# One interleaved program for projection, attention and output of each mixer in the second block

## The reference, cut to what matters

```
proj = rms_norm(x, n1) @ w_in_l                     # 1024 -> 2560
qa, ka, va, qd, kd, vd, qc, kc, vc = split(proj)    # 256x3, 384x3, 384, 128, 128
qa, ka, qd, kd, qc, kc: rms_norm per head of 64     # with gains
qd, kd: rotary on 16 of 64; qc, kc: axial rotary on all 64
out_a = softmax(qa ka^T + bias from rpb) va         # 4 heads, neighbourhood
out_d = softmax(qd kd^T + log of multiplicity) vd   # 6 heads, dilated windows
out_c = softmax(qc kc^T) vc                         # 6 heads over 2 key heads
mix = concat(rms_norm(out_a), rms_norm(out_d), rms_norm(out_c))
x = x + mix @ w_out_l                               # 1024 -> 1024
```

## Time and profile before

| | |
|---|---|
| median of 3 runs | 1798.05 us (1797.01 to 1801.28) |
| the profiled execution: its time | 1802.4 us |
| the profiled execution: its span | 1800.6 us |
| mean granted clock of TensorE in it | 0.971 of full |
| busy share: TensorE, VectorE, ScalarE, GpSimd | 93%, 57%, 47%, 8% |

### The profile page before, as it was taken

How to read it: one execution, slowest core, us unless ns; L and a number is a source line. 1 busy time by engine, 2 the same in 40 slices (tenths; PEclk the granted TensorE clock), 3 DMA queues, 4 the chain that set the end, 5 groups by cost and what they waited for, 6 DMA issues and landing times.

```text
span 1800.6 us, 28794 instructions
## 1 busy us (share of the span) xinstructions
PE 1683.3 (93%) x11689; PEld 1526.4 (85%) x11689; DVE 1024.3 (57%) x1303; ACT 844.1 (47%) x1185; POOL 152.2 (8%) x190
## 2 busy tenths in 40 slices
PE   7999997899999999998999998968999997899998
PEld 7999885799989999886689997946999987579997
DVE  6444555544455444668654445675655566666654
ACT  5344465444435443436544444564544454644443
POOL 0000011000000000230000002530000038000000
PEclk9999997999999999999999999989999998999999
DMA  7555441355545555432045555511545564025452
GB/s 267 187 186 187 162 153 61 133 194 186 186 164 188 185 181 181 154 118 71 25 176 187 183 179 139 201 48 47 187 166 197 182 180 163 1 100 190 177 188 92
DMA packets 40546, 276.85 MB, mean 154 GB/s; under 512 B 5505, under 2 KB 6290, under 8 KB 7570
## 3 DMA queue, kind: packets, MB, share of 16 engines
q1 hardware_dynamic: 39010, 271.00, 42.5%
q0 software_dynamic: 1456, 4.72, 1.7%
HBM read 274.65 MB, written 1.05 MB: 153 GB/s over the span
## 4 chain that ended last, share of the span: by engine, by line
PE 80%; DVE 9%; ACT 5%; POOL 3%; issue 2%; DMA 0%; SPq 0%; POOLq 0%; DVEq 0%; ACTq 0%
PE bank L661 19%; PE bank L642 14%; PE bank L644 14%; PE bank L643 14%; PE bank L622 5%; PE bank L573 3%; PE bank L574 3%; PE bank L575 3%; DVE w_lo L1356 2%; ACT prob L1178 1%; POOL proj L500 1%; ACT work L1064 1%; DVE prob L1536 1%; PE bank L718 1%; ACT w_hi L1054 1%
## 5 line engine op out<-in xcount | busy, mean ns | idle before, releaser
L1356 DVE TENSOR_TENSOR w_lo<-raw,w_hi 128x2048 fp32r<-128x2048 f32 x255 | 587.4, 2308 | 533.9 <-ACT w_hi L1054 533.2
L1054 ACT ACTIVATE w_hi<-raw 128x2048 fp32r<-128x2048 f32 x255 | 487.3, 1917 | 552.2 <-PE bank L644 404.0
L642 PE MATMUL bank<-xt_hi,w_hi 128*128 128x256 f32 x2112 | 599.8, 284 | 5.7 <-DVE xt_lo L1388 5.7
L644 PE MATMUL bank<-xt_hi,w_lo 128*128 128x256 f32 x2112 | 598.2, 283 | 0.0
L643 PE MATMUL bank<-xt_lo,w_hi 128*128 128x256 f32 x2112 | 598.1, 283 | 0.0
L642 PEld LDWEIGHTS bank<-xt_hi,w_hi 128*128 128x128 f32 x2112 | 405.6, 192 | 9.4 <-issue 5.0
L643 PEld LDWEIGHTS bank<-xt_lo,w_hi 128*128 128x128 f32 x2112 | 405.7, 192 | 2.5
L644 PEld LDWEIGHTS bank<-xt_hi,w_lo 128*128 128x128 f32 x2112 | 405.7, 192 | 0.0
L661 PE MATMUL bank<-w_hi,h_hi 128*128 128x512 f32 x528 | 208.3, 395 | 0.2
L661 PE MATMUL bank<-w_hi,h_lo 128*128 128x512 f32 x528 | 208.5, 395 | 0.0
L661 PE MATMUL bank<-w_lo,h_hi 128*128 128x512 f32 x528 | 208.2, 394 | 0.0
(11 more groups left out here) (301 smaller groups left out, 1635.2 us busy)
## 6 DMA issues: line engine op xcount, KB each, us to landing
raw<-in_stream SPq DMA_DIRECT2D x255, 1024.0 KB, 4.9
work<-in_rpb POOLq DMA_DIRECT2D x32, 64.0 KB, 3.7
X<-in_x SPq DMA_DIRECT2D x2, 512.0 KB, 4.0
prob<-in_cmp_w POOLq DMA_DIRECT2D x1, 1024.0 KB, 5.3
O<-in_cmp_w POOLq DMA_DIRECT2D x1, 1024.0 KB, 7.0
out<-X SPq DMA_DIRECT2D x1, 1024.0 KB, 4.0
cst<-in_consts SPq DMA_DIRECT2D x1, 776.0 KB, 5.9
O<-in_final_gain POOLq DMA_DIRECT2D x1, 512.0 KB, 4.2
```

What stands on the lines that cost most here:

```text
L642: pe.matmul(o, w_hi[:, sl, cols], xt_hi[:, k, :], start=(k == 0), stop=False)
L644: ins = pe.matmul(o, w_lo[:, sl, cols], xt_hi[:, k, :], start=False, stop=(k == KD - 1))
L1054: act.activation(w_hi[:, sl, :], raw[:, sl, :], ACT.Copy).then_inc(hi_done, 1)
L1356: dve.tensor_tensor(w_lo[:, sl, :], raw[:, sl, :], w_hi[:, sl, :].bitcast(F32), ALU.subtract).then_inc(lo_done, 1)
```

## The change

`project`, `feature_major`, `attention` and `mix_out` of the second block are replaced by one `sec_mixer(l)` on each of the three engines, an order of small steps. It contains:

- **Column order.** `SEC_ORDER` becomes gqa queries and keys, dilated queries and keys, gqa values, dilated values, then the neighbourhood kind. The first kind is complete after block 1, the second after block 4, the third after block 8.
- **Interleaving.** After five whole blocks the two first feature groups are transposed, and gqa pair 0 starts. The other five blocks are cut into half blocks (24 matmuls, one half of the tokens), between which stand the scores, transposes and values of the gqa and dilated pairs. The output tiles (12 matmuls each, `out_k`) stand between the last pairs; `out_last` does tiles 6 and 7.
- **Banks.** Projection in banks 0 and 1, scores in 4 and 5 (two instead of four), transposed probabilities in bank 6 (one instead of two, with four instead of two destinations in `KT`), attention output and square sums both in bank 7.
- **Roots.** `Sqrt` on ScalarE and reciprocal on VectorE are replaced by `Ln`, then `Exp` with scale -0.5, on ScalarE, and one Newton step on VectorE, for the three kinds of heads and for the three kinds of output (there with a Newton step that was not there before).
- **Heads.** VectorE does token half 0 of the first kind (gqa), GpSimd everything else; `mask_bias` stands between the second and the third kind.
- **Square sums** are taken for a kind at once, three (or two) matmuls behind each other.

The functions that the diff leaves out do what those of before did, on the banks named. Cut to its core (indentation reduced):

```diff
-SEC_ORDER = ("qa", "ka", "qd", "kd", "qc", "kc", "va", "vd", "vc")
-QA, KA, QD, KDL, QC, KC, VA, VD, VC = (sum(SEC_W[m] for m in SEC_ORDER[:i]) for i in range(9))
+SEC_ORDER = ("qc", "kc", "qd", "kd", "vc", "vd", "qa", "ka", "va")
+QC, KC, QD, KDL, VC, VD, QA, KA, VA = (sum(SEC_W[m] for m in SEC_ORDER[:i]) for i in range(9))
...
+SEC_TILES = [QC + P * i for i in range(3)] + [KC] + [QD + P * i for i in range(3)] + [KDL + P * i for i in range(3)] + \
+[QA, QA + P, KA, KA + P]
+SEC_DST = (10, None, 4, 6, 8, 0, 2)
+SEC_FT_BANK = (2, 3, 2, 3, 2, 4, 5)
...
+SEC_KINDS = ((QC, 8, 0, 1, 384), (QD, 12, 8, 4, 384), (QA, 8, 20, 8, 256))
+SEC_S, SEC_T, SEC_O = (4, 5), 6, 7
...
+    def half(c, t):
+        if t == 0:
+            pe.wait_ge(lo_done, u0 + c + 1)
+            if c >= 2:
+                pe.wait_ge(pj_evac, p0 + c - 1)
...
+    def transposes(g):
+        if g == 0:
+            pe.wait_ge(ft_ready_d, 4 + l)
+            pe.wait_ge(ft_ready_p, 4 + 3 * l)
+        elif g == 2:
+            pe.wait_ge(ft_ready_p, 5 + 3 * l)
+            pe.wait_ge(ft_a, a0 + 1)
+        elif g == 3:
+            pe.wait_ge(ft_a, a0 + 2)
+            pe.wait_ge(ft_d, d0 + 1)
+        elif g == 4:
+            pe.wait_ge(ft_d, d0 + 2)
+        elif g == 5:
+            pe.wait_ge(ft_ready_p, 6 + 3 * l)
+            pe.wait_ge(exp_done, 2 * (j0 + 12))
...
+    def scores(m):
+        if m in (0, 3, 6):
+            pe.wait_ge(ft_a, a0 + (2, 3, 4)[m // 3])
+            pe.wait_ge(ft_d, d0 + (1, 3, 4)[m // 3])
+        if m == 6:
+            pe.wait_ge(na_ready, l + 1)
+        if m:
+            pe.wait_ge(exp_done, 2 * (j0 + 2 * m))
...
+    def turn_p(i):
+        pe.wait_ge(p_scaled, j0 + i + 1)
+        if i:
+            pe.wait_ge(pt_evac, j0 + i)
...
+    for c in range(5):
+        half(c, 0)
+        half(c, 1)
+    transposes(0)
+    transposes(1)
+    half(5, 0)
+    scores(0)
+    half(5, 1)
+    half(6, 0)
+    scores(1)
+    turn_p(0)
+    half(6, 1)
+    turn_p(1)
+    half(7, 0)
+    scores(2)
+    turn_p(2)
+    values(0)
+    turn_p(3)
+    half(7, 1)
+    transposes(2)
+    transposes(3)
+    half(8, 0)
+    transposes(4)
+    scores(3)
+    turn_p(4)
+    values(1)
+    turn_p(5)
+    half(8, 1)
+    scores(4)
+    turn_p(6)
+    values(2)
+    turn_p(7)
+    half(9, 0)
+    square_sums(0)
+    half(9, 1)
+    scores(5)
+    turn_p(8)
+    values(3)
+    turn_p(9)
+    out_k(0)
+    transposes(5)
+    transposes(6)
+    turn_p(10)
+    values(4)
+    turn_p(11)
+    scores(6)
+    out_k(1)
+    values(5)
+    scores(7)
+    square_sums(1)
+    turn_p(12)
+    out_k(2)
+    turn_p(13)
+    turn_p(14)
+    values(6)
+    turn_p(15)
+    out_k(3)
+    values(7)
+    square_sums(2)
+    out_k(4)
+    out_k(5)
+    out_last()
...
+    def head_root(n):
+        act.wait_ge(e_ms, 3 * l + n + 1)
+        act.activation(head_rms(rstd, n), head_rms(ms, n), ACT.Ln).then_inc(e_ln, 1)
+        act.wait_ge(e_ln, 3 * l + n + 1)
+        act.activation(head_rms(rstd, n), head_rms(rstd, n), ACT.Exp, scale=-0.5).then_inc(e_rt, 1)
...
+    def out_root(kind):
+        act.wait_ge(e_m, 3 * l + kind + 1)
+        act.activation(o_norm[:, kind, :], o_ms, ACT.Ln).then_inc(e_ml, 1)
+        act.wait_ge(e_ml, 3 * l + kind + 1)
+        act.activation(o_norm[:, kind, :], o_norm[:, kind, :], ACT.Exp, scale=-0.5).then_inc(e_mr, 1)
...
+    evac(0)
+    split(u0 + 3)
+    evac(1)
+    head_squares(0)
+    split(u0 + 4)
+    head_root(0)
+    evac(2)
+    split(u0 + 5)
+    evac(3)
+    split(u0 + 6)
+    evac(4)
+    head_squares(1)
+    tiles(0)
+    tiles(1)
+    split(u0 + 7)
+    head_root(1)
+    exponentials(0)
+    evac(5)
+    split(u0 + 8)
+    turned(0)
+    exponentials(1)
+    evac(6)
+    turned(1)
+    split(u0 + 9)
+    turned(2)
+    exponentials(2)
+    turned(3)
+    pair_out(0)
+    evac(7)
+    tiles(3)
+    split(u0 + 10)
+    turned(4)
+    exponentials(3)
+    turned(5)
+    pair_out(1)
+    evac(8)
+    head_squares(2)
+    split(u0 + 11)
+    turned(6)
+    exponentials(4)
+    turned(7)
+    pair_out(2)
+    head_root(2)
+    evac(9)
+    split(u0 + 12)
+    out_root(0)
+    turned(8)
+    exponentials(5)
+    turned(9)
+    pair_out(3)
+    out_hi(0)
+    out_hi(1)
+    tiles(5)
+    turned(10)
+    turned(11)
+    pair_out(4)
+    exponentials(6)
+    out_hi(2)
+    pair_out(5)
+    split(u0 + 13)
+    turned(12)
+    out_root(1)
+    exponentials(7)
+    turned(13)
+    out_hi(3)
+    turned(14)
+    pair_out(6)
+    turned(15)
+    out_hi(4)
+    out_hi(5)
+    pair_out(7)
+    out_root(2)
+    out_hi(6)
+    out_hi(7)
+    split(u0 + 14)
...
+    def newton(r, q, mean_sq, ins_sem):
+        link(dve.tensor_tensor(q, r, r, ALU.mult))
+        link(dve.tensor_tensor(q, q, mean_sq, ALU.mult))
+        link(dve.tensor_scalar(q, q, -0.5, 1.5, ALU.mult, ALU.add))
+        ins = dve.tensor_tensor(r, r, q, ALU.mult)
...
+    split(u0 + 3)
+    head_sums(0)
+    split(u0 + 4)
+    head_root(0)
+    sec_heads(dve, link, 0, 0, l, KT[:, 2048:2560])
+    dve.sem_inc(ft_ready_d, 1)
+    split(u0 + 5)
+    split(u0 + 6)
+    tiles(1)
+    head_sums(1)
+    split(u0 + 7)
+    head_root(1)
+    maxima(0)
+    scale(0)
+    split(u0 + 8)
+    maxima(1)
+    scale(1)
+    split(u0 + 9)
+    maxima(2)
+    tiles(2)
+    scale(2)
+    split(u0 + 10)
+    tiles(4)
+    maxima(3)
+    scale(3)
+    head_sums(2)
+    maxima(4)
+    split(u0 + 11)
+    head_root(2)
+    scale(4)
+    out_mean(0)
+    maxima(5)
+    split(u0 + 12)
+    out_root(0)
+    out_scale(0)
+    out_scale(1)
+    scale(5)
+    out_lo(0)
+    out_scale(2)
+    out_lo(1)
+    tiles(6)
+    maxima(6)
+    out_lo(2)
+    scale(6)
+    split(u0 + 13)
+    maxima(7)
+    out_mean(1)
+    out_root(1)
+    out_scale(3)
+    scale(7)
+    out_scale(4)
+    out_lo(3)
+    out_scale(5)
+    out_lo(4)
+    out_lo(5)
+    out_mean(2)
+    out_root(2)
+    out_scale(6)
+    out_scale(7)
+    out_lo(6)
+    out_lo(7)
+    split(u0 + 14)
...
-        for t in ((0, 1) if n < 2 else (1,)):
-            sec_heads(pool, link, n, t, l, QT[:, 3072:4096])
+        for t in ((1,), (0, 1), (0, 1))[n]:
+            sec_heads(pool, link, n, t, l, KT[:, 2560:3072])
         pool.sem_inc(ft_ready_p, 1)
-    mask_bias(l)
+        if n == 1:
+            mask_bias(l)
     norm(8 + 2 * l)
```

More of the change, by code:

```diff
@@ L748, in values @@
                     pair, br = m // per, m % per
-                    if br == 0 and pair >= 1 and stage[:3] == "sec":
-                        pe.wait_ge(o_copied, 8 * int(stage[3]) + pair)
-                    if br == 0 and pair >= 2 and stage[:3] != "sec":
+                    if br == 0 and pair >= 2:
                         pe.wait_ge(xtl, 8 * TURN["m0" if stage == "mla" else "m1"] + (4 if stage == "mla" else 0)
                                    + pair - 1)
-                    ob = bank[4 if stage[:3] == "sec" else 4 + pair % 2]
+                    ob = bank[4 + pair % 2]
                     if stage == "nsa" and br == 0:
@@ L767, in values @@
                                 pe.matmul(dst, job["v"](0), pts_of(i, 0, S), start=first, stop=False)
-                            elif job["causal"]:
+                            else:
                                 pe.matmul(dst[:, P:S], job["v"](1), pts_of(i, S, S + P), start=False,
                                           stop=last).then_inc(pv_done, 1)
-                            else:
-                                pe.matmul(dst, job["v"](1), pts_of(i, S, 2 * S), start=False,
-                                          stop=last).then_inc(pv_done, 1)
-                def square_sums(place):
-                    l = int(stage[3])
-                    pe.wait_ge(o_copied, 8 * l + place + 1)
-                    kind = kind_of(place)
-                    if place == 3:
-                        pe.wait_ge(e_m, 3 * l + 1)
-                    dst = bank[5 if kind < 2 else 6][:, 0:S]
-                    pe.matmul(dst, const("ones"), o_sq[:, place % 2, :], start=place in (0, 3, 6),
-                              stop=place in (2, 5, 7)).then_inc(o_sum, 1)
                 scores(0)
@@ L1155, in feature_major @@
                         for to, src in nsa_keys(bank[ft_bank(stage, g)], g):
-                            ins = act.activation(to, src, ACT.Copy)
-                        ins.then_inc(ft_a, 1)
-                    elif stage[:3] == "sec" and g == 6:
-                        ps = bank[ft_bank(stage, g)]
-                        act.activation(qk[:, 12, :], ps[:, 0:S], ACT.Copy)
-                        for to, src in gqa_keys_low(ps):
                             ins = act.activation(to, src, ACT.Copy)
@@ L1324, in _ @@
                 norm(6 + 2 * l)
-                project(f"sec{l}", U[f"sec_in{l}"], SEC_BLOCKS, lambda c: sec_rms(l, c))
-                feature_major(f"sec{l}")
-                attention(f"sec{l}")
-                for place in range(KD):
-                    if place in (0, 4):
```

(25 more changed lines are left out.)

353 lines of the change are left out of this document (237 added, 116 removed).

## The result

The changed kernel takes 1808.11 us (median of 5 runs, 1805.56 to 1811.14) beside 1798.54 of the kernel before: a ratio of 1.0052, 95% interval 1.0034 to 1.0069. It is slower, by 9.6 us. The forecast was 1795.0, and its own case reached to 1803.4.

The account below looks back on a forecast made before the run. TensorE, busy 93% of the span, bounds it. Per mixer 116.0 us work + 22.65 waits + 5.0 clock = 143.65 (144.0 walked) against 145.7; two save 3.4, less 0.4: 1798.05 - 3.0 = 1795.0 us, range 1780 to 1809.

Parts of the forecast that it names:

- its own case: Whole kernel about even, overlap gains and queue-order waits nearly cancelling: 1792.7 to 1803.4 us, chance 0.41.
- the walk: Three engines' in-order programs laid side by side through one mixer; T counts us from the projection's first matmul, ending at 144.0.
- scores 3: Wait for feature group 4 on VectorE, behind split 10: until T 65.35, 2.25 us lost.
- output tile 0: Wait for its low part from VectorE until T 95.05, 3.65 us lost; VectorE, not the table loads, the limit.
- transposes 14: Wait for pair 7's exponentials, queued behind the second output root; scaled at T 122.25, 4.05 us lost.
- the transposes of the second kind: After block 7, wait for GpSimd's heads until T 58.7, 2.35 us lost.
- transposes 9: Wait for copy 8, behind evacuation 9, split 12 and first output root with two loads: T 90.9, 4.0 us lost.
- rival 2: Clearly faster: clock holds, 5 us a mixer back, and VectorE's heads take 5.5 for 7.7 us; 1782 us, chance 0.29.
- Rival 3: Ln and Exp share one table, so root waits shrink, 9 us a mixer: 1777 us, chance 0.05.
- 0.4 in all: Allowance for POOL slowing VectorE operations beside it; two such meetings on the path priced at up to 1.4 us.
- Rival 4: Slower: clock also falls mid-mixer, T 56 to 65; two falls cost +5 us a mixer, 1805 us, chance 0.25.
- -1.7 us a mixer: Forecast mixer change: last matmul at 144.0 in the walk against 145.7 us before; 3.4 us for two.

Follow-up runs that it names:

- tiles first: Changed kernel with VectorE's copy of the last feature-major tile moved ahead of split 10: 1800.36 us, ratio 1.0014 to the kernel before.
- the four orders: Changed kernel, Ln and Exp kept, with mask in VectorE's idle time, last feature tile's copy earlier, output tile 0 first, unit 14 split early: 1792.91 us, ratio 0.9959.

## Why the prediction was wrong

**What held.** Much of the walk: of its five waits above 2 us, three stand where they were put, before scores 3 (4.31 us for 2.25), output tile 0 (5.39 for 3.65) and transposes 14 (3.91 for 4.05), and the 12 loads a mixer of 1.28 us are there. The other two do not: the transposes of the second kind waited 0.41 us for 2.35, and the 4.0 before transposes 9 came as 0.48, 1.61 and 1.17, spread over transposes 8, values 3 and transposes 9. Up to the transposes of the second kind the walk was within 1.5 us (T 57.24 against 58.7). The waits listed in it add up to 22.75, not 22.65, which changes nothing. The heads on VectorE took 8.1 us, so rival 2 had no ground there. Rival 3 (one table for Ln and Exp) is out.

**First step that failed: GpSimd beside VectorE.** The text took "0.4 in all" and called the mask hidden, because nothing waited for its result. It cost through the engine beside it: one pair of scalings went from 0.62 to 3.59 us, those of probabilities 8 and 9 from 1.24 to 3.67. I had priced such a meeting from two splits, which there lost little. With the mask out of the way 5 us came back.

**Second: the clock in the middle.** Rival 4 had the mechanism, and priced it as a pair of falls. One came: scores 3 stood at T 65.95, only 0.6 later than predicted, but after 4.31 us of waiting in place of 2.25 with the transposes done earlier, and the work behind ran at half clock. Transposes 7 then stood 3.0 us later than in the walk (T 78.55 against 75.55, which is counted back from its end of block 9). I had charged only waits of 4 us with a fall, taken 2.25 for this one, and it grew over that line by the step above. Nor did a fall need 4 us here: with tiles first, 2.10 us at this place was still followed by half clock in one mixer.

**Third: output tile 0**, T 99.86 against 95.05. Of these 4.8 us, 2.4 are the stretched scalings of probabilities 8 and 9, which stand ahead of maxima 5; the rest was there before them. Taking the stretch away at that place did not pay, since it moved to the next operations; so what is shown is the stretch, and not that its cure is worth 2.4 us. From maxima 5 on VectorE was the limit, as predicted, and took 9.2 us without a pause for the 9.65 of the walk. But "the loads are not the limit" was wrong: ahead of the scalings VectorE had waited 2.98 us for the third kind's root with its two loads, and with the roots left out tile 0 started 2.7 us earlier behind the norm (0.8 of it already at scores 3).

**Fourth: the end of the mixer.** The walk stopped at the last matmul (144.0 predicted, about 148.6 measured; 145.7 before). The 0.8 us of a longer gap at the norm and the half clock in the feed-forward parts (0.6 and 2.0) were in no term. The gap hangs on output root 2 and on split 14 behind it: it is 1.56 us with either moved or shortened. So does the first feed-forward part: 193.8 us in five of the six traces with the gap of 1.56, 194.4 or more in all nine with 2.35 us or more. Of the second part's 2.0 us at most some 0.6 do, for six traces with the long gap have 197.9 to 198.0 us there and only three have 199.4; what decides between these is open.

**The size of the loads.** In the walk they were on the path at transposes 9 and 14, 2.6 us each, all together some 9 us a mixer if one table served (rival 3). Taking away 5 of 12 gained 12 us in two mixers and what follows them, by the estimate above more than half of it the clock. The walk had this right in kind: a change that keeps Sqrt would have come out even with the kernel before, which was measured (0.9987).

Two of the signs named in advance did not come: the last matmul (T 142 to 147; it ended at 148.6) and the pause of about 4 us before transposes 9. The forecast's -1.7 us a mixer thus became +3.7 and +3.1, with 2.6 outside the mixers. That the interleaving itself can pay is shown by the four orders, 0.9959 with the same operations on every engine.

## What to carry to other kernels

A filler on GpSimd is hidden only if VectorE stands idle at that time or does something that the meeting leaves alone (here work on PSUM banks, sums and reciprocals, and not splits, scalings and products); place it by the neighbour's timeline, not by when its result is needed. In an interleaved program look first at what each in-order queue does right ahead of TensorE's largest wait, and move what nobody needs yet (a split, a mask, a copy for later) behind it: here four such moves of a line or two gave 17 us. And count a wait with the half clock behind it, and follow the walk past the end of the stage that you change.
